# A two-block model on one core: softmax steps of two units placed in a row on VectorE and ScalarE, four PSUM banks emptied between two exponentials, and recurrent steps and squares of the second mixer moved by a beat

## The reference

```
y_a = rg_lru(x_lru) * gelu(gate)        # conv of 4 taps, sigmoid gates, h = a*h + b over the tokens
y_b = chunk_attention(q, k, v)          # 8 heads of 64, a band of chunks, a relative bias
y   = concat(rmsnorm(y_a), rmsnorm(y_b));  x = x + y @ w_out
```

## Time and profile before

| what | value |
|---|---|
| median of 3 runs | 1719.15 us (1716.31 to 1720.82) |
| the profiled execution | 1716.58 us, its span 1715.3 us, TensorE clock 0.983 of full speed |
| PE busy | 1602.2 us (93%) |
| the chain that ended last | PE 70%, DMA 12%, ACT 9%, DVE 5%, issue 3% |
| DVE, ACT, POOL busy | 931.4 us (54%), 686.8 us (40%), 553.3 us (32%) |
| PE idle before line 620, ended by ACT line 1987 | 7.3 us in 3 waits, the longest 4.2 us |
| PE idle before line 468, ended by DVE line 1688 | 4.2 us in 3 waits, the longest 3.5 us |
| PE idle before line 468, ended by ACT line 2082 | 2.7 us, one wait |

### The profile page before, as it was taken

How to read it: one execution, slowest core, us unless ns; L and a number is a source line. 1 busy time by engine, 2 the same in 40 slices (tenths; PEclk the granted TensorE clock), 3 DMA queues, 4 the chain that set the end, 5 groups by cost and what they waited for, 6 DMA issues and landing times.

```text
span 1715.3 us, 23299 instructions
## 1 busy us (share of the span) xinstructions
PE 1602.2 (93%) x9505; PEld 1270.1 (74%) x9505; DVE 931.4 (54%) x1462; ACT 686.8 (40%) x1021; POOL 553.3 (32%) x323
## 2 busy tenths in 40 slices
PE   7998999999999996998899999999999779999997
PEld 5777845454545443887879999999999668888886
DVE  5864512111101112665444588688623898888886
ACT  6554411110100101565443444344444984555453
POOL 3211100000000001322122343443554997777671
PEclk9999999999999999998999999999999999999999
DMA  7432989999999999533334455555566118999994
GB/s 277 148 99 90 383 339 421 421 421 421 421 422 421 421 421 360 191 123 135 123 123 148 152 187 186 183 187 189 199 221 216 68 49 311 352 352 344 355 339 153
DMA packets 99344, 444.81 MB, mean 259 GB/s; under 512 B 11152, under 2 KB 19856, under 8 KB 57632
## 3 DMA queue, kind: packets, MB, share of 16 engines
q1 hardware_dynamic: 86256, 404.90, 63.1%
q0 software_dynamic: 11264, 33.60, 5.3%
q10 hardware_dynamic: 1712, 4.76, 0.7%
HBM read 435.26 MB, written 7.86 MB: 258 GB/s over the span
## 4 chain that ended last, share of the span: by engine, by line
PE 70%; DMA 12%; ACT 9%; DVE 5%; issue 3%; POOL 0%; ACTq 0%; SPq 0%; DVEq 0%
PE ps L650 12%; PE ps L468 11%; PE ps L470 11%; PE ps L469 11%; PE ps L1089 10%; PE ps L1082 7%; DMA fix<-in_w_up 5%; DMA big<-in_w_up 5%; PE ps L673 2%; ACT y L2336 2%; DMA hl<-in_w_up 2%; DVE fix_parts L1120 1%; ACT fix_parts L1944 1%; PE ps L633 1%; PE ps L715 1%
## 5 line engine op out<-in xcount | busy, mean ns | idle before, releaser
L2376 POOL TENSOR_TENSOR fix_parts<-fix,fix_parts 128x512 fp32r<-128x512 f32 x59 | 144.7, 2454 | 726.7 <-ACT fix_parts L1944 726.7
L470 PE MATMUL ps<-hh_parts,fix_parts 128*128 128x256 f32 x1120 | 317.9, 284 | 0.0
L1120 DVE TENSOR_TENSOR fix_parts<-fix,fix_parts 128x1536 fp32r<-128x1536 f32 (+1 forms) x84 | 171.9, 2046 | 113.5 <-ACT fix_parts L1944 109.4
L468 PE MATMUL ps<-hh_parts,fix_parts 128*128 128x256 f32 x768 | 220.5, 287 | 10.2 <-issue 5.9
L469 PE MATMUL ps<-hl_parts,fix_parts 128*128 128x256 f32 x768 | 218.9, 285 | 0.0
L470 PEld LDWEIGHTS ps<-hh_parts,fix_parts 128*128 128x128 f32 x1120 | 215.7, 193 | 0.0
L650 PE MATMUL ps<-big 128*64 128x512 f32 x784 | 197.9, 594 | 11.0 <-DMA big<-in_w_up 5.7
L1944 ACT ACTIVATE fix_parts<-fix 128x2048 fp32r<-128x2048 f32 x84 | 160.6, 1915 | 64.0 <-PE ps L1089 52.8
L650 PEld LDWEIGHTS ps<-big 128*64 128x64 f32 x784 | 68.8, 137 | 129.0 <-issue 128.2
L468 PEld LDWEIGHTS ps<-hh_parts,fix_parts 128*128 128x128 f32 x768 | 148.8, 194 | 11.8 <-issue 11.8
L650 PE MATMUL ps<-fix,big 128*64 128x512 f32 x528 | 143.5, 594 | 6.0 <-DMA fix<-in_w_up 3.6
(11 more groups left out here) (399 smaller groups left out, 3793.1 us busy)
## 6 DMA issues: line engine op xcount, KB each, us to landing
fix<-in_expert_u SPq DMA_DIRECT2D x64, 1024.0 KB
fix<-in_expert_v SPq DMA_DIRECT2D x38, 1024.0 KB
big<-in_w_up SPq DMA_DIRECT2D x35, 1024.0 KB, 23.2
big<-in_w_gate SPq DMA_DIRECT2D x33, 1024.0 KB, 20.5
big<-in_w_down SPq DMA_DIRECT2D x30, 1024.0 KB, 23.1
big<-in_expert_v SPq DMA_DIRECT2D x26, 1024.0 KB
fix<-in_w_gate SPq DMA_DIRECT2D x23, 1024.0 KB, 22.2
fix<-in_w_down SPq DMA_DIRECT2D x22, 1024.0 KB, 25.1
```

The source lines that it names most:

```text
L468: pe.matmul(o, l[0], r[0], start=first, stop=False)
L470: return pe.matmul(o, l[1], r[0], start=False, stop=last)
L1120: nc.vector.tensor_tensor(m.fr(x[:, 0:end]), x[:, 0:end], m.fr(hi[:, 0:end]).bitcast(F32), ALU.subtract).then_inc(s.lo_v, 1)
L2376: nc.gpsimd.tensor_tensor(m.fr(x[:, at:2048]), x[:, at:2048], m.fr(hi[:, at:2048]).bitcast(F32), ALU.subtract).then_inc(s.lo_g, 1)
```

## The change

A new kind of step, E, is ScalarE's exponentials; S is from now on TensorE's and VectorE's part alone. S and E can so stand at different beats.

- Mixer 1: S of unit 5 goes from beat 26 to 25, and its exponentials too. The exponentials of unit 7 go from beat 30 to beat 32, and on ScalarE beat 32 comes before the `act_high` of the next tile; so they come right behind the four copies of the memory keys.
- Mixer 2: `lru` 1 goes from beat 10 to 11 and `lru` 2 from 11 to 12. S and exponentials of unit 11 go from beat 18 to 17; `hssq` goes from 17 to 18, `lrusum` from 18 to 19, behind R of unit 10.

No instruction is added or taken away other than those that the order decides (loads of ScalarE's tables).

```diff
@@ BEATS1
-    13: [("S", 0)], 14: [("S", 1)], 15: ...
-    18: [("S", 2), ("S", 3), ("forget", 0)], 20: ...
+    13: [("S", 0), ("E", 0)], 14: [("S", 1), ("E", 1)], 15: ...
+    18: [("S", 2), ("S", 3), ("E", 2), ("E", 3), ("forget", 0)], 20: ...
-    25: [("S", 4)], 26: [("S", 5)], 27: [("R", 4)], 28: [("R", 5), ("P", 4)], 29: [("P", 5)], 30: [("S", 6), ("S", 7)],
-    32: [("R", 6), ("R", 7)], 33: [("P", 6), ("P", 7)], 34: [("outfturn", 0), ("group", 1)],
+    25: [("S", 4), ("S", 5), ("E", 4), ("E", 5)], 27: [("R", 4)], 28: [("R", 5), ("P", 4)], 29: [("P", 5)],
+    30: [("S", 6), ("S", 7), ("E", 6)], 32: [("E", 7), ("R", 6), ("R", 7)], 33: [("P", 6), ("P", 7)], 34: [("outfturn", 0), ("group", 1)],
@@ BEATS2
-    9: [("lru", 0)], 10: [("lru", 1)], 11: [("lru", 2)],
-    13: [("S", 8)], 14: [("S", 9)], 15: [("R", 8)], 16: [("R", 9), ("gelu", 0), ("lru", 3)], 17: [("hssq", 0), ("S", 10)],
-    18: [("lrusum", 0), ("S", 11)], 19: [("R", 10)], 20: [("R", 11), ("P", 8), ("P", 9)], 21: [("P", 10), ("P", 11)],
+    9: [("lru", 0)], 11: [("lru", 1)], 12: [("lru", 2)],
+    13: [("S", 8), ("E", 8)], 14: [("S", 9), ("E", 9)], 15: [("R", 8)], 16: [("R", 9), ("gelu", 0), ("lru", 3)],
+    17: [("S", 10), ("S", 11), ("E", 10), ("E", 11)], 18: [("hssq", 0)], 19: [("R", 10), ("lrusum", 0)],
+    20: [("R", 11), ("P", 8), ("P", 9)], 21: [("P", 10), ("P", 11)],
@@ scalar_first, beat          (the same in scalar_second)
-            elif what == "S":
+            elif what == "E":
                 act_exps(nc, m, s, o, u)
@@ scalar_first
     leave_features(f["w_km0"], m.KMT[0])
     tile = f["w_vm0"]
+    beat(32)
     high(t.split[tile] + AHEAD)
-    beat(32)
     beat(33)
```

More of the change, by code:

```diff
@@ L45 @@
     8: [("qkroot", 1), ("rope", 1)], 9: [("qkscale", 1)], 11: [("memnorm", 0)], 12: [("qkturn", 1)],
-    13: [("S", 0)], 14: [("S", 1)], 15: [("R", 0), ("soft", 0)], 16: [("R", 1), ("P", 0), ("qksq", 0)], 17: [("P", 1)],
-    18: [("S", 2), ("S", 3), ("forget", 0)], 20: [("R", 2), ("R", 3), ("qksq", 1)], 21: [("P", 2), ("P", 3), ("qkroot", 0)],
+    13: [("S", 0), ("E", 0)], 14: [("S", 1), ("E", 1)], 15: [("R", 0), ("soft", 0)], 16: [("R", 1), ("P", 0), ("qksq", 0)], 17: [("P", 1)],
+    18: [("S", 2), ("S", 3), ("E", 2), ("E", 3), ("forget", 0)], 20: [("R", 2), ("R", 3), ("qksq", 1)], 21: [("P", 2), ("P", 3), ("qkroot", 0)],
     22: [("memturn", 0)], 23: [("outdturn", 0), ("group", 0), ("qkscale", 0)], 24: [("qkturn", 0)],
-    25: [("S", 4)], 26: [("S", 5)], 27: [("R", 4)], 28: [("R", 5), ("P", 4)], 29: [("P", 5)], 30: [("S", 6), ("S", 7)],
-    32: [("R", 6), ("R", 7)], 33: [("P", 6), ("P", 7)], 34: [("outfturn", 0), ("group", 1)],
+    25: [("S", 4), ("S", 5), ("E", 4), ("E", 5)], 27: [("R", 4)], 28: [("R", 5), ("P", 4)], 29: [("P", 5)],
+    30: [("S", 6), ("S", 7), ("E", 6)], 32: [("E", 7), ("R", 6), ("R", 7)], 33: [("P", 6), ("P", 7)], 34: [("outfturn", 0), ("group", 1)],
 }
@@ L2208, in beat @@
         for what, u in beats.get(i, ()):
-            if what == "S":
+            if what == "E":
                 act_exps(nc, m, s, o, u)
```

## The result

| | median | runs |
|---|---|---|
| before | 1718.2 us | 4 (1716.31 to 1720.82) |
| after | 1707.04 us | 4 (1706.21 to 1713.08) |
| ratio | 0.9942 | 95% interval 0.9915 to 0.9968 |

The change gained 11.2 us by these medians; a second set (8 runs after, 13 before) says 0.9952 (0.9935 to 0.9969), 8.8 us by its medians. The forecast was 7.4 us and a time of 1711.8.

The account below looks back on a forecast made before the run. The stream of expert weights was taken to bound the expert stage, its start set by mixer 1. Mixer 1's 4.4 plus mixer 2's 3.0 gave 7.4 us off the median 1719.15: 1711.8 us, range 1707 to 1718.5.

Parts of the forecast that it names:

- Unit 5: Mixer 1: its turn stops waiting, the stall moves to the P of unit 4; gain 2.4 us, not 4.15.
- The port: Both mixers: DVE's rest and POOL's part contend for one port; loss 0 or 1.1 us, taken as 0.55 each.
- the lower case of 0.8: Mixer 2, recurrent steps: the 3.46 us stall gives 1.9, only 0.8 with the port lost to POOL; 1.35 taken.
- The clock in mixer 1: Behind the 4.15 us wait: still falls, but dense products come 2.4 us sooner; gain 0.9, bounds 0 and 3.4.
- Unit 7: Mixer 1: memory-key copies ahead of its exponentials start PE at 159.5, not 161.08; gain 1.6 us, exponentials covered.
- The stream does not swallow it: Experts: mixer 1's saving starts the weight stream sooner, one for one; rival that only mixer 2 counts, 1716.2 us, chance 0.12.
- Squares: Mixer 2: turn of unit 11 stops waiting, `outl` waits 2.5 us for DVE's last rest; gain 3.6, 3.0 after the port.
- the rival of half clock through both P: Mixer 2: slow clock lasts until P of unit 11 ends at 797.5; mixer 2 loses 3.1, time 1717.8, chance 0.15.
- both clock terms: Half clock: 0.9 us gained in mixer 1, 1.7 us lost in mixer 2 as `outl` starts.
- the case in which the clock falls at neither place: Rival, both mixers: 3.4 instead of 0.9 and 1.7 more, time 1707.5 us, chance 0.10.
- The slower rival: Half clock in both mixers, about 8 us more than before; sum -3.2 with the port lost twice, 1722.3 us, chance 0.06.

Follow-up runs that it names:

- second set: The unchanged change measured again against the kernel before, 8 runs after and 13 before: median 1708.83 us, ratio 0.9952.
- mixer 2 alone: Kernel before with only the mixer 2 edits (recurrent steps a beat later, squares behind both exponentials): 1715.4 us, ratio 0.9988.
- unit 5 alone: Kernel before with only unit 5's softmax moved to beat 25: 1715.97 us (1 run).
- recurrent steps alone: Kernel before with only the recurrent steps of mixer 2 a beat later: 1713.27 us (1 run).
- squares alone: Kernel before with only squares and their sums moved behind the exponentials of units 10 and 11: 1719.43 us (1 run).
- after twice: The changed kernel, profiled in two sets against the kernel before: 1707.04 us, ratio 0.9942, and 1708.83 us, ratio 0.9952.
- mixer 1 alone: Kernel before with only the mixer 1 edits (unit 5's softmax, unit 7's exponentials): 1711.75 us, ratio 0.9967.
- unit 7 alone: Kernel before with only unit 7's exponentials moved behind the four copies of the memory keys: 1714.89 us (1 run).
- the four built on after: Changed kernel plus useless products, copy early, squares early, or both of the last two: ratios to before 0.9929, 0.9926, 0.9936, 0.9915.
- useless products: Changed kernel plus 16 unread products behind the turn of unit 10 and 5 behind the sums: 1706.24 us, ratio to before 0.9929.
- squares early: Changed kernel with the squares ahead of the exponentials of units 10 and 11, sums at beat 18: 1704.19 us, ratio to before 0.9936.
- copy early: Changed kernel with DVE's copy of unit 4's probabilities ahead of the rest of the next weight tile: 1702.49 us, ratio to before 0.9926.
- with both moved: Changed kernel with unit 4's copy ahead of the weight tile's rest and the squares ahead of the exponentials: 1701.71 us, ratio to before 0.9915.

## Why the prediction was right

**Unit 5: right.** P of unit 4 began 16.74 us behind the scores of unit 4 (138.57), before it was 19.10 (141.14): 2.4, the number forecast, and the stall moved to where the prediction put it. DVE's copy came at 137.81.

**The port: both ways seen.** In mixer 1 DVE started first and lost nothing (0 of the 0 to 1.1), in mixer 2 POOL did and DVE lost 1.1: the gate's wait gave 1.2, and S of unit 8 came 0.7 sooner behind q (40.60 against 41.33), which is the lower case of 0.8 and not the 1.9. All eight profiles with the recurrent steps a beat later have POOL first there by 0.02 to 0.03, DVE's rest at 2.88 and the gate's wait at 2.22 to 2.24, and all eight with unit 5 moved have DVE first in mixer 1 and its rest at 1.76. So it was open to the prediction, but it is no toss-up from run to run. The Trainium skill (SBUF — State Buffer, Who interferes with whom) says that the order of issue decides which of the two is blocked. The four rows agree: 0.03 or 0.04 us of lead was enough.

**The clock in mixer 1: the step that failed.** It was to give 0.9; in the prediction's own sum it took 0.6. The gain of the stretch, 3.5, is 1.7 of unit 7 and 2.4 of unit 5, and so -0.6 is left for the clock. Half clock lasted 6.8 us as before, but began at 139.0 instead of 139.8, that is over the whole P of unit 4 (3.09 us for what takes 1.97 at full clock). "The next dense products come sooner" did not shorten it. Nor did it cost more than before: the turn of unit 5, which ran under half clock before (1.82 us), now stands ahead of it (1.03), and that part is in the 2.4 already, in the forecast as in the measurement. So the half clock itself cost the same as before, and the term beside the 2.4 should have been -0.6.

**Unit 7: right in its mechanism, too small in its worth.** The wait went from 2.71 to 0.99 (1.7; forecast 1.6), the exponentials were covered. But the 2.71 us wait seems to have a second price that the one trace of before does not show (its clock is 1.00 in the wait and behind it, from 161.0 to 169.4). Half clock of 3.4 or 6.8 us follows it in four of the five profiles that have it (mixer 2 alone, unit 5 alone, recurrent steps alone, squares alone; not before). It follows in none of the eight with 0.99 to 1.04 (after twice, mixer 1 alone, unit 7 alone, and the four built on after). In the trace of mixer 2 alone it makes 2.8 us, in that of the recurrent steps nothing beyond what was saved at 139. Unit 5 alone has it and unit 7 alone has not, so it goes with the wait and not with the other edit. Over the five profiles it averages 4.1 us, worth 2.0 by my estimate (half of it), which fits the 5.7 us by medians against 3.5 by the trace of mixer 1 alone. With one profile for most kernels it is likely, not shown.

**The stream does not swallow it: right.** 3.7 us sooner at the first expert weights, 3.9 sooner at q; 541.7 us between against 541.9, and 539.8 to 542.1 in all thirteen profiles. What sets the pace of the experts is less sure than the prediction had it: PE is busy 235.43 of the first 237 us as well. The argument only needs that the start moves the end.

**Squares: right in what is late, wrong in what ends it.** The 3.85 us wait, the missing table load and the free turn of unit 11 came as forecast. But `outl` did not start behind DVE's rests (they end at 774.67) but behind PE's own sums, at 776.05: they ran at half clock and took 3.58 us, where before took 1.84. The prediction had them done before the rests; the half clock that it did expect it put behind them. Mixer 2's 3.05 became 1.2, some 1.9 less: 0.55 for the port, 1.3 for the sums (`outl` starts 1.4 behind the rests, 0.1 was forecast), 0.2 behind `outl` (13.76 us to the loads, forecast 13.6), and back the 0.1 by which the rests came before their date. At full clock the sums would have taken 1.6 less (1.95, as with the useless products) and been done ahead of the rests. So the rival of half clock through both P was half true: 10.2 us of it, but begun at 770.5, over the wait, and ended at 780.7, before the P of unit 8.

**The time.** By the first pair of traces the change is 4.7, forecast 7.4; by medians 8.8 and 11.2. All thirteen profiles narrow this. In the four with the old mixer 1 (before, mixer 2, recurrent steps and squares alone) it took 47.44 to 51.77 us, mean 49.23; in the five with both of its edits and no more (after twice, mixer 1 alone, useless products, squares early) 43.33 to 43.97, mean 43.72: 5.5 gained, forecast 4.4. In the four with the old mixer 2 that took 83.46 to 84.37, mean 83.71 (before, mixer 1, unit 5 and unit 7 alone); in the four with both of its edits and no more (after twice, mixer 2 alone, copy early) 81.66 to 82.33, mean 82.07: 1.6 gained, forecast 3.0. Together 7.1, so the forecast sum is near, with too little in mixer 1 and too much in mixer 2: too much gain in both clock terms stood against too little worth for `vm0`'s wait. That these cancel is luck. What lies outside the two stretches took 1578.0 to 1585.4 us in these profiles, so one span against another cannot show a gain of this size.

That the first median lies in the range is luck as well. It is inside by 0.04 us (1707.04 against 1707), and that end of the range was set by the case in which the clock falls at neither place; it fell at both. The second set's 1708.83 lies 1.8 inside. The forecast also counted down from 1719.15, while the four medians of before are 1717.2 to 1718.2, so 1 to 2 us of the distance are the starting point's. The slower rival had its condition met (half clock at both places), but not its size: 8 us more than before were needed, and the two mixers had 17.0 us of it against 20.4.

## What to carry to other kernels

A step moved ahead of a wait hands the wait on: write down what the engine does next and what that waits for, as with the copy of unit 4 and the squares, and move that too. In mixer 2 that was worth more in the stretch (6.3 us) than the change itself (1.2, by all profiles 1.6), and in mixer 1 about as much (5.5 and, with both moved, 4.2, against 3.5 and by all profiles 5.5). Price a stall on TensorE with what the clock does behind it, and take that from several profiles: the same wait had 0, 3.4 or 6.8 us of half clock behind it. Where one trace gives less than the medians, profile the halves of the change apart: each is a further profile of the old code of the other half.

## What the hardware did that I had not expected

- The sixteen one-column products of the sums took 3.58 us at half clock and 1.95 at full: small as they are, they decided when `outl` could start.
- With 3.92 us of useless products in a wait of 3.85, and 5 more behind it, the clock did not fall in the one profile of this, and it paid for them in the stretch: 3.96 us saved, 1.24 given.
- Code that is the same up to there had half clock of different length behind the same wait of 4.15 us at the turn of unit 5: 6.8 us in before, 3.4 with the recurrent steps alone.
- ACT's load of tables costs its 1.28 us and no gap on either side where nothing else is waited for: in before it starts at 776.27, at once behind the rounding ahead of it, and the root starts at 777.57, 0.02 behind its end. In after the root waits until 776.22 for PE, not for the load (done at 775.45).
- Which of DVE and POOL takes the port first, by 0.02 to 0.05 us, was the same at each of the two places in all eight profiles that have it.
